# A fused two-block transformer kernel: two steps of dense work ahead of the first attention, its gate chunks spread differently, and both ends of the expert stage reordered

## The reference, cut to what matters

```python
def first_block(x, ...):
    h = rmsnorm(x, norm_mix_g)
    x = x + token_mixer(h, ...)          # gated short convolution beside forgetting attention
    h2 = rmsnorm(x, norm_ffn_g)
    x = x + hier_moe(h2, ...)
    return rmsnorm(x, norm_final_g)

def forgetting_attention(q, k, v, f_logit, b_forget):     # 16 heads of 64, blocks of 128 queries
    ...
        s = jnp.einsum('bqhd,bkhd->bhqk', qblk, kp).astype(jnp.float32) * scale
        s = s + (cum[:, :, qs:qe, None] - cum[:, :, None, :qe])
        s = jnp.where(s_pos <= t_pos, s, -jnp.inf)
        p = jax.nn.softmax(s, axis=-1).astype(v.dtype)
        outs.append(jnp.einsum('bhqk,bkhd->bqhd', p, vp))

def token_mixer(...):
    ...
    m = jax.nn.sigmoid(g_conv) * y_conv + jax.nn.sigmoid(g_att) * y_att
    return m @ w_out

def hier_moe(hf, ...):    # 512 tokens, 4 groups of 8 experts, the two best of one group
    ...
    def expert_block(args):
        xb, e = args
        a = xb @ w_e_gate[e]
        u = xb @ w_e_up[e]
        return (jax.nn.silu(a) * u) @ w_e_down[e]
```

## Time and profile before

| | |
|---|---|
| median of 3 runs | 1891.53 us (1890.48 to 1893.15) |
| the profiled execution | 1886.33 us, its span 1884.2 us, mean granted TensorE clock 0.972 |
| TensorE, VectorE, ScalarE, GpSimd busy | 92%, 61%, 52%, 12% of the span |
| chain that ended last | TensorE 67%, VectorE 11%, DMA 9%, issue 8%, ScalarE 4% |
| first attention | about 273 to 525 us |
| expert stage, first gather to last scatter | about 643 to 1161 us |

### The profile page before, as it was taken

One profiled execution on the slowest core, in us unless ns is written; L12 is line 12 of the kernel. 1 busy time (PEld: TensorE's weight loads), 2 busy tenths in 40 slices (PEclk: granted clock), 3 DMA queues, 4 the chain that ended last, 5 costly groups with the idle time before them and its releaser, 6 DMA issues.

```text
span 1884.2 us, 23249 instructions
## 1 busy us (share of the span) xinstructions
PE 1742.8 (92%) x8654; PEld 1419.8 (75%) x8654; DVE 1157.4 (61%) x1650; ACT 984.6 (52%) x1366; POOL 234.0 (12%) x174
## 2 busy tenths in 40 slices
PE   6999999999999599999999994899999999998999
PEld 5888878888788477777777773788788888887567
DVE  3543435444564599999999995771647643537452
ACT  4222234444432399999888984554353223557330
POOL 0000001010000124444232331010010000000000
PEclk9999999999999699999999997899999999999799
DMA  6755357434144699999999995232022332223001
GB/s 143 107 97 79 112 90 62 69 58 66 39 145 182 218 385 421 421 422 422 422 421 422 421 373 196 79 111 91 23 90 90 120 113 96 94 61 102 1 1 67
DMA packets 127043, 326.47 MB, mean 173 GB/s; under 512 B 8176, under 2 KB 80624, under 8 KB 118768
## 3 DMA queue, kind: packets, MB, share of 16 engines
q1 hardware_dynamic: 121360, 315.85, 51.1%
q0 software_dynamic: 5168, 8.92, 1.3%
q10 hardware_dynamic: 432, 0.56, 0.1%
HBM read 319.02 MB, written 15.21 MB: 177 GB/s over the span
## 4 chain that ended last, share of the span: by engine, by line
PE 67%; DVE 11%; DMA 9%; issue 8%; ACT 4%; POOL 0%; DVEq 0%; SPq 0%; POOLq 0%; ACTq 0%
PE bank L1422 14%; PE bank L1424 13%; PE bank L1423 13%; DMA down<-in_w_e_down 6%; PE turned L1422 3%; PE turned L1423 3%; PE turned L1424 3%; DVE down_lo L2351 2%; PE bank L1757 2%; DVE gate_lo L2351 2%; DVE up_lo L2351 2%; PE bank L1502 2%; PE bank L1597 2%; PE bank L1970 1%; DMA gate<-in_w_e_gate 1%
## 5 line engine op out<-in xcount | busy, mean ns | idle before, releaser
L2004 DVE TENSOR_TENSOR w_lo<-w_raw,w_hi 128x2048 fp32r<-128x2048 f32 (+2 forms) x76 | 163.8, 2157 | 286.9 <-ACT w_hi L884 286.8
L884 ACT ACTIVATE w_hi<-w_raw 128x2048 fp32r<-128x2048 f32 (+3 forms) x132 | 169.4, 1306 | 279.6 <-DMA w_raw<-in_w_in 75.6
L1422 PE MATMUL bank<-h1T_hi,w_hi 128*128 128x512 f32 x376 | 152.3, 405 | 0.0
L1424 PE MATMUL bank<-h1T_hi,w_lo 128*128 128x512 f32 x376 | 148.4, 395 | 0.0
L1423 PE MATMUL bank<-h1T_lo,w_hi 128*128 128x512 f32 x376 | 147.7, 393 | 0.0
L2351 DVE TENSOR_TENSOR down_lo<-down,down_hi 128x2048 fp32r<-128x2048 f32 x62 | 139.0, 2280 | 2.3 <-ACT down_hi L884 2.2
L2351 DVE TENSOR_TENSOR gate_lo<-gate,gate_hi 128x2048 fp32r<-128x2048 f32 x64 | 128.9, 2017 | 0.4 <-ACT gate_hi L884 0.3
L2351 DVE TENSOR_TENSOR up_lo<-up,up_hi 128x2048 fp32r<-128x2048 f32 x64 | 126.5, 2017 | 1.2 <-ACT up_hi L884 1.1
L884 ACT ACTIVATE down_hi<-down 128x2048 fp32r<-128x2048 f32 x62 | 115.1, 1905 | 16.2 <-DMA down<-in_w_e_down 16.2
L815 POOL COPY put_row<-table 64x1 int32 (+1 forms) x32 | 88.2, 2755 | 260.3 <-DVE ys L2386 258.1
L884 ACT ACTIVATE gate_hi<-gate 128x2048 fp32r<-128x2048 f32 x64 | 108.7, 1700 | 20.1 <-DMA h_dram<-h_tok 10.5
(11 more groups left out here) (673 smaller groups left out, 4462.8 us busy)
## 6 DMA issues: line engine op xcount, KB each, us to landing
gate<-in_w_e_gate SPq DMA_DIRECT2D x32, 2048.0 KB, 17.0
up<-in_w_e_up SPq DMA_DIRECT2D x32, 2048.0 KB, 17.3
down<-in_w_e_down SPq DMA_DIRECT2D x32, 2048.0 KB, 18.3
w_raw<-in_w_in SPq DMA_DIRECT2D x24, 1024.0 KB, 9.0
w_raw<-in_a_w_in SPq DMA_DIRECT2D x20, 1024.0 KB, 5.3
w_raw<-in_w_in SPq DMA_DIRECT2D x16, 512.0 KB, 9.0
w_raw<-in_a_w_out SPq DMA_DIRECT2D x8, 1024.0 KB, 5.0
w_raw<-in_c_w_in SPq DMA_DIRECT2D x6, 1024.0 KB, 5.1
```

The costliest lines, as they stand in the source:

```text
L884: return nc.scalar.activation(out, in_, ACT.Copy, scale=scale)
L1422: pe.matmul(out, sh, mh, start=start, stop=False)
L1424: return pe.matmul(out, sl, mh, start=False, stop=stop)
L2004: V.tensor_tensor(ring_view(w_lo, n), ring_view(raw, n), ring_view(w_hi, n).bitcast(F32), ALU.subtract)\
```

## The change

In the first attention:
- Two steps without an item (AHEAD = 2) stand in front of item 0 in window 0, so its 32 dense chunks are spread over ten steps: three chunks of q1(1) in each of the first two. Transposes and products follow their scores with the same lag in items.
- Window 6 gets gatt(6) as well, 24 chunks in 8 items, so that k1(7) is complete in the step of item 53 instead of 55. Window 7 keeps gatt(7) alone: 8 chunks over the 8 items and 3 empty steps, one each at items 57, 58, 60, 61, 62 and in three of the four steps behind item 63. Pieces of the next weight slice (att_out) are split at items 53 and 54 instead of 56 and 57.

At the start of the expert stage:
- h2 is scaled in place, so its store does not share a buffer with gate_hi. ACT makes the high parts of expert 0's gate, up and down right behind the router's exponentials. DVE makes down_low(0) behind up_low(0).
- SP issues the stores of h2 ahead of the load of up(1), and the load of gate(1) waits until they have landed.
- DVE writes the first `get_row` itself, ahead of the table; POOL gathers at once. `twice` comes ahead of the router's late values.

At its end:
- The last down weights go to a buffer of their own, `down_last`, which SP loads after gate_done(NE - 1), and DVE makes `down_lo_last` in two halves with the last gated product between them.
- ACT makes hx_high(30) behind the copy of the last up sum, between the halves of `down_hi_last`.
- POOL copies `put_row` for expert 31 and reads the overflow values before it waits for that expert's y. DVE splits the second block's first weights behind `moe_done`.

```diff
 LAG = 3
+AHEAD = 2
...
         elif w < KC - 2:
             beside += [("gatt", w), ("gatt", w + 1)]
+        else:
+            beside += [("gatt", w)]
+        items = [8 * w + e for e in range(8)]
+        if w == 0:
+            items = [None] * AHEAD + items
         elif w == KC - 1:
-            beside += [("gatt", w - 1), ("gatt", w)]
+            items = items + [None] * LAG
...
-    steps += [[None, [], [], []] for _ in range(LAG + 1)]
+    steps.append([None, [], [], []])
...
-        k = t - LAG
+        k = t - AHEAD - LAG
...
             sp.dma_start(ring_down[1][:, :, :], down_src(1)).then_inc(down_landed[1], 16)
+            for tt in range(TT):
+                sp.wait_ge(sem("h2_rows"), tt + 1)
+                sp.dma_start(h2_dram[tt * P:(tt + 1) * P, :], h2g[:, tt, :]).then_inc(h2_stored, 16)
             sp.wait_ge(results, order[("logits", 0)] + 1)
             sp.dma_start(ring_up[1][:, :, :], up_src(1)).then_inc(up_landed[1], 16)
...
+            sp.wait_ge(h2_stored, 16 * TT)
             sp.dma_start(ring_gate[1][:, :, :], gate_src(1)).then_inc(gate_landed[1], 16)
-            sp.wait_ge(sem("routed"), 1)
+            sp.wait_ge(sem("over_made"), 1)
...
             next_down((None, NE - 4), 0)
-            next_down((None, NE - 3), 1)
+            sp.wait_ge(gate_done, NE - 1)
+            sp.dma_start(down_last[:, :, :], down_src(NE - 1)).then_inc(sem("last_down_landed"), 16)
...
-            get_pair((None, 0))
+            pool.wait_ge(sem("get_ready"), 2)
+            pool.sem_inc(turn, 1)
+            gather()
+            pool.wait_ge(sem("table_made"), 1)
...
-            for e in range(NE - 2, NE):
-                put((None, e), e % 2)
+            put((None, NE - 2), 0)
+
+            pool.wait_ge(scattered, 16 * NE)
+            pool.sem_inc(turn, 1)
+            nc.gpsimd.tensor_copy(put_row[1][:, :], table[:, NE - 1:NE, 1]).then_inc(sem("put_ready"), 1)
+            pool.wait_ge(sem("put_ready"), NE)
+            count, _ = over_values(pool)
+            pool.wait_ge(y_made, NE)
+            pool.sem_inc(turn, 1)
+            scatter(1)
...
-            hx_high(expert(last, -1))
             act.wait_ge(gate_done, NE)
-            act.wait_ge(down_landed[1], 8 * NE)
+            act.wait_ge(sem("last_down_landed"), 16)
...
                 if half == 0:
                     up_copy(last)
+                    hx_high(expert(last, -1))
...
+            for x in range(2):
+                V.tensor_copy(get_row[half_rows(x), :], slot_g[:, x:x + 1]).then_inc(sem("get_ready"), 1)
...
             up_low((None, 0), 0)
+            down_low((None, 0), 0)
             x_low((None, 1), 1)
             gate_low((None, 1), 1)
             up_low((None, 1), 1)
-            down_low((None, 0), 0)
...
             dve.wait_ge(moe_done, 1)
+            split(slices1, n_slices)
```

More of the change, by code:

```diff
@@ L125, in head_steps @@
             beside += [("gatt", w), ("gatt", w + 1)]
+        else:
[3 more added lines that the diff above has]
+            items = [None] * AHEAD + items
         elif w == KC - 1:
-            beside += [("gatt", w - 1), ("gatt", w)]
+            items = items + [None] * LAG
         groups = [g for key in beside for g in groups_of(key)]
         weight = [1 if key[0] == "v1" else 2 for key, _ in groups]
-        place = [(sum(weight[:k + 1]) * 8 - 1) // sum(weight) for k in range(len(groups))]
-        for e in range(8):
+        place = [(sum(weight[:k + 1]) * len(items) - 1) // sum(weight) for k in range(len(groups))]
+        for e, item in enumerate(items):
             here = [g for g, p in zip(groups, place) if p == e]
@@ L138, in head_steps @@
                     begun.append(before)
-            steps.append([8 * w + e, here, done, begun])
-    steps += [[None, [], [], []] for _ in range(LAG + 1)]
+            steps.append([item, here, done, begun])
+    steps.append([None, [], [], []])
     plan, pieces = [], []
@@ L834, in _ @@
             nc.gpsimd.memset(pool_mark[:, 0:1], 0).then_inc(sem("ovf_free"), 1)
-            count, _ = over_values(pool)
             with pool.If(count > 0):
@@ L1071, in _ @@
             for tt in range(TT):
-                copy(h2_tok[:, tt, :], h2g[:, tt, :], rstd[:, tt:tt + 1]).then_inc(sem("h2_rows"), 1)
+                copy(h2g[:, tt, :], h2g[:, tt, :], rstd[:, tt:tt + 1]).then_inc(sem("h2_rows"), 1)
             act.wait_ge(sem("router_e1"), 1)
@@ L1158, in _ @@
             gate_copy(last)
[L1159 removed]
             act.wait_ge(gate_done, NE)
[L1161 removed]
+            act.wait_ge(sem("last_down_landed"), 16)
             for half in range(2):
                 cs = slice(half * FC // 2, (half + 1) * FC // 2)
[L1164 removed]
+                copy(down_hi_last[:, cs, :], down_last[:, cs, :]).then_inc(down_hi_made, 1)
                 if half == 0:
                     up_copy(last)
+                    hx_high(expert(last, -1))
             silu(last)
@@ L1787, in _ @@
                     pe.wait_ge(down_lo_made, 2 * (NE - 1) + 1 + f // (FC // 2))
-                for w in (down_hi_last, down_lo[1]):
+                for w in (down_hi_last, down_lo_last):
                     for a in range(2):
@@ L2331, in _ @@
             step(V.scalar_tensor_tensor(out=slot_g[:, :], in0=slot_g[:, :], scalar=-float(SEQ), in1=slot_u[:, :], op0=ALU.mult, op1=ALU.add))
+            for x in range(2):
+                V.tensor_copy(get_row[half_rows(x), :], slot_g[:, x:x + 1]).then_inc(sem("get_ready"), 1)
             V.tensor_copy(table[:, :, 1], slot_u[:, :])
             V.tensor_copy(table[:, :, 0], slot_g[:, :]).then_inc(sem("table_made"), 1)
-            step(V.tensor_tensor(ovt[:, :, :], incl[:, :].unsqueeze(1).to_broadcast([P, 16, NE]),
-                                 iota[:, 0:16].unsqueeze(2).to_broadcast([P, 16, NE]), ALU.is_le))
-            step(V.tensor_reduce(ovs[:, 0:16], ovt[:, :, :], AX_X, ALU.add))
-            step(V.tensor_scalar(ovs[:, 0:16], ovs[:, 0:16], float(NE - 1), None, ALU.min))
-            step(V.tensor_copy(ovs[:, 16:17], incl[:, NE - 1:NE]))
-            V.tensor_copy(over[:, 0:17], ovs[:, 0:17]).then_inc(sem("over_made"), 1)
-            dve.wait_ge(sem("router_e4"), 1)
-            step(V.tensor_scalar(den, e2, 1.0, None, ALU.add))
-            step(V.reciprocal(den, den))
-            step(V.tensor_tensor(tok_w[:, 0, :], den, g_val, ALU.mult))
-            step(V.tensor_tensor(tok_w[:, 1, :], tok_w[:, 0, :], e2, ALU.mult))
             def low_half(lo, raw_, hi, e, half, hi_made_, lo_made_):
@@ L2400, in _ @@
             V.tensor_tensor(twice[:, :], ident[:, 0:CAP], ident[:, CAP:2 * CAP], ALU.add).then_inc(sem("routed"), 1)
+            step(V.tensor_tensor(ovt[:, :, :], incl[:, :].unsqueeze(1).to_broadcast([P, 16, NE]),
+                                 iota[:, 0:16].unsqueeze(2).to_broadcast([P, 16, NE]), ALU.is_le))
+            step(V.tensor_reduce(ovs[:, 0:16], ovt[:, :, :], AX_X, ALU.add))
+            step(V.tensor_scalar(ovs[:, 0:16], ovs[:, 0:16], float(NE - 1), None, ALU.min))
+            step(V.tensor_copy(ovs[:, 16:17], incl[:, NE - 1:NE]))
+            V.tensor_copy(over[:, 0:17], ovs[:, 0:17]).then_inc(sem("over_made"), 1)
+            dve.wait_ge(sem("router_e4"), 1)
+            step(V.tensor_scalar(den, e2, 1.0, None, ALU.add))
+            step(V.reciprocal(den, den))
+            step(V.tensor_tensor(tok_w[:, 0, :], den, g_val, ALU.mult))
+            step(V.tensor_tensor(tok_w[:, 1, :], tok_w[:, 0, :], e2, ALU.mult))
             gate_low((None, 0), 0)
@@ L2413, in _ @@
             hx_low(expert(last, -1))
-            for half in range(2):
-                low_half(down_lo[1], ring_down[1], down_hi_last, last, half, down_hi_made, down_lo_made)
+            low_half(down_lo_last, down_last, down_hi_last, last, 0, down_hi_made, down_lo_made)
             dve.wait_ge(hx_lo_made, NE - 1)
@@ L2419, in _ @@
             V.tensor_tensor(hxs_last[:, :, CAP:], hx[:, :, :], hxs_last[:, :, 0:CAP].bitcast(F32), ALU.subtract).then_inc(hx_lo_made, 1)
+            low_half(down_lo_last, down_last, down_hi_last, last, 1, down_hi_made, down_lo_made)
             y_sum(expert(last, -1), 0)
@@ L2425, in _ @@
             ins.then_inc(y_made, 1)
-            split(slices1, n_slices)
             count, _ = over_values(dve)
```

17 lines of the change are left out of this document (6 added, 11 removed).

## The result

| | before | after |
|---|---|---|
| median of the runs | 1891.01 us (1888.42 to 1893.15, 4 runs) | 1863.97 us (1863.39 to 1864.46, 4 runs) |
| profiled execution | 1886.33 us | 1863.39 us |
| ratio after / before | | 0.9866, 95% interval 0.9855 to 0.9878 |

The change saves 27.0 us by the medians and 25.3 us (23.1 to 27.4) by the ratio; forecast were 20.9, and the measured time lies 2 us under the range. The two profiled executions differ by 22.9 us only. All measurements of this study together hold 81 executions of the kernel before: 1884.2 to 1893.3 us, median 1888.9. Against that the change saves 24.9.

What follows compares the result with a forecast made beforehand. The prediction took TensorE, busy for 92% of the span, as the bound, with the weight stream on top in the expert stage. 11.1 + 1.8 + 8.0 = 20.9 us off 1891.53 made 1870.6, range 1866 to 1881.

Steps and rivals of the forecast that it cites:

- part A: First attention: moved chunks take away idle and lower clock; gain 11.1 us, bounds 9.2 to 12.2.
- It lies 5.2 below the median of the runs, and against that: Whole time: profiled 1886.33 gives 1865.4; against the runs' median, 1891.53 - 20.9 = 1870.6 us.
- first two places: Before the first scores and before item 56: idle and lower clock go, gains 5.8 and 4.9 us.
- Part B: Expert stage's start: gather and first ring refill come earlier; gain 1.8 us, bounds 0 and 2.9.
- Part C: Expert stage's end: last down product 4.8 us earlier, then 3.2 behind it; gain 8.0, bounds 4.5 and 9.
- The clock's term: Last sums and expert 30's down: no fall of the clock expected; 3.1 us too many at 0.64, 2.5 taken.
- The tail: From the last sum of ys to the y loads: 3.7 of 6.9 us remain, gain 3.2.
- 1, the stream takes the start's gain: Expert stage: the full weight stream takes the start's gain, leaving 0 of it, 1872.4 us; chance 0.12.
- 2, thinned steps starve: Attention from item 56 on: thinned steps wait and the clock falls, 7.1 us more, 1877.7; chance 0.13.
- 3, the clock falls at the end all the same: Experts' end: clock falls because of the 0.8 us idle that stay; 2.5 less, 1873.1 us; chance 0.07.
- 4, the slower side: Loop over experts: GpSimd's chain passes 31 us, VectorE's sum waits each period; 1900.6 at 1.0 us a period; chance 0.02.
- 5: First attention: TensorE's waits have another cause that comes last, most of the gain stays away, 1880 us; chance 0.03.

Runs made afterwards that it cites:

- the kernel before again: The kernel before, no edit, measured again: ratio 1.0008, median 1890.31 us over 12 runs.
- B alone: Kernel before with only the edits of the expert stage's start: ratio 0.9985, 2.8 us faster, median 1885.80.
- C alone: Kernel before with only the edits of the expert stage's end, GpSimd's included: ratio 0.9958, 7.9 us faster, median 1881.46.
- stores late: Kernel before with the expert start's edits, but h2's stores behind the load of up(1), as before: ratio 1.0016, median 1891.69.
- second trace of before: Profiled execution of the unedited kernel before, from its repeated measurement: 1892.09 us.
- A alone: Kernel before with only the first attention's table changed: ratio 0.9926, 14.0 us faster, median 1875.16.
- AHEAD alone: Kernel before with only the two steps in front (AHEAD = 2), windows 6 and 7 as before: ratio 0.9970, median 1882.88.
- The gate chunks: Changed kernel's first attention table with no step in front (AHEAD = 0), everything else as in the kernel before: ratio 0.9964, median 1881.84.
- The filling of the end: Kernel before, window 7's 16 chunks over 8 items and three empty steps: ratio 0.9995. Changed kernel without end filling: 1866.17 us, 2.2 slower.
- the experiment with down_low(0): Changed kernel with VectorE's down_low(0) back behind up_low(1): ratio to before 0.9870, median 1864.00 us.
- the late load: Changed kernel with the last down weights' load issued after expert 29's down product, still into its own buffer: ratio to before 0.9865, median 1863.18.

## Why the prediction was wrong, step by step

**Direction and parts: right. The sum was too small, and what it was taken from too high.** The forecast is 1891.53 - 20.9 = 1870.6, and 1863.97 was measured, 6.6 less. Two steps failed.

The first is part A's price of the clock's falls, some 3 of the 6.6 us (B and C were 0.4 and 0.7 short). The falls were read from one execution: 1.7 us behind the first scores, 1.7 behind item 56, and none at the attention's end, which was priced at +0.4 from its idle alone. That execution took 365.49 us from first scores to router table; the four other traces of the same attention (the kernel before again, B alone, C alone, stores late) took 368.4 to 368.6. In the second trace of before, the 2.9 us lie all behind item 56, as the fall at the end. In the other three, 0.8 to 0.9 lie ahead of item 56, where the fall behind the first scores costs about 2.7 and not 1.7, and 2.2 behind it, of which the clock's fall at the end makes 1.4 to 1.6. The change takes all of this away in nearly every trace (354.3 and 354.4 in four of the changed kernel and its variants), so the attention gives about 14.1, and A alone measures 14.0 (11.1 to 16.8), not 11.1.

The second is "It lies 5.2 below the median of the runs, and against that": the median was of three runs, and it lay high. Over 81 executions it is 1888.9, so only 2.6 of the 5.2 are there to be added, and the other 2.6 are the rest of the miss. From 1888.9 to 1863.97 are 24.9 us, 4.0 more than 20.9. That three runs fell high is chance; so is the start, which differs by up to 3.0 us over all these traces (first scores at 273.27 to 276.24, apart already at the first dense product) in a part that the change does not touch.

**Part A, first two places: right.** Both waits and both falls went. AHEAD alone gives 5.7 for a forecast 5.8. The gate chunks give 6.8 (4.2 to 9.4) for 5.3, which does not tell the two forecasts apart. The filling of the end gives 0.9 in the kernel before and 1.5 to 2.2 in the changed one, above the +0.4 that was taken and about its upper bound of +1.5.

**Part B: mechanism right, 2.2 in the trace for 1.8.** The first refill alone counts; the experiment with down_low(0) shows it (2.8 us of lead, no time). From the router table to the first refill, seven traces with the old start take 19.0 in the mean (17.6 to 19.6) and eight with the new one 17.0 (16.4 to 17.5). The rest of the size: the gather goes 1.5 us earlier behind the table, not 1.7, and the time until its rows are turned was taken as unchanged, 5.3 us, where it is 4.1. Over the traces it is 4.5 to 6.5 with the old start, 4.1 to 4.5 with the new one, and 8.9 with the stores late.

**Part C: 8.7 for 8.0, and one cause wrong.** That the last down weights "may be asked for at about 1118 instead of 1127" stood first among the reasons, and it does nothing: the late load landed at the same time. The landing of 1135.5 was right (1122.1 in the changed kernel, 13.4 us earlier, as its first refill is 13.3 earlier), since the load queues behind the one before. What gives 2.3 of the 2.4 us of earlier sums is hx_high's place on ScalarE. The Trainium skill ("DMA: Bandwidth & Descriptors", "Latency and other measured facts") ties the two slower DMA engines to descriptors that are made in software. These weight loads go over a hardware queue (`hardware_dynamic` in the profile), so the rule was misapplied; the runs show the queueing and no slower engine. The clock's term was 3.2 for 2.5 taken and 3.1 reckoned: I took off 0.6 for VectorE's deliveries, and TensorE waited for none. It was 3.2 in this pair of traces; three of nine with the wait lose only 1.6. The tail: 3.0 for 3.2.

**Rivals.** 1, the stream takes the start's gain: no, part B alone measures 2.8 (0.8 to 4.7), and 2.2 of lead at the first refill is there at the last one too. 2, thinned steps starve: the end has 1.35 us of waits where before had 2, and no fall in the changed kernel's trace (the late load's has one, 1.7 us). 3, the clock falls at the end all the same: no, 0.73 us of wait left it at 1.00. 4, the slower side: periods unchanged (444.4 us from first to last refill of a gate before, 444.5 after). 5: no.

What stays open is why the clock falls at the attention's end in some executions and not in others with the same waits. The sorting by the wait before item 56 rests on seven and nine traces, no more. Open too is why the falls behind the first scores and behind the last sums are of two lengths for the same wait.

## What to carry to other kernels

Before a gain is reckoned from one profile, hold that execution against the spread of the runs, and take more than three runs for it: here three lay 2.6 us high and the profile 2.6 us low. If it lies low, some stall of the typical execution may be missing from it: a place with short waits whose clock stayed up is the first suspect, and it is worth its own term. In these traces the waits of TensorE of 2.0 to 4.3 us cost their length and 1.4 to 3.2 us of lower clock behind them, so a few chunks of independent work in front are worth more than the idle that they fill. When a load queues behind another, asking for it earlier moves nothing; look at what stands in front of its consumer instead. And look twice before a large load is released together with a small gather that TensorE waits for.

## What the runs showed of the hardware that was not expected

- The same idle pattern (waits of 0.35, 0.24, 0.57 and 0.77 us at the attention's end) was followed by a granted clock of 1.00 in one execution and of 0.5 over 6 us in another of the same kernel.
- A 2 MB load asked for 9.9 us later landed within 0.2 us of the same time, 5.0 us behind its predecessor.
- A gather of 128 rows took 4.1 to 6.5 us until TensorE turned them in fifteen traces, and 8.9 in the one with a 2 MB load issued 1.0 us ahead.
- Behind a wait of 2.0 us the granted clock was 0.83 in the 4 us from 276. Behind the 0.73 us before the last sums it was 1.00 in the changed kernel, and the stretch took the same 9.0 us in all seven traces that have this wait.
- The same wait of 3.15 us before the last sums was followed by a lower clock that cost 3.2 us in six traces and 1.6 in three.
